# Up projection of a streaming-encoder block: channels by tokens against tokens by channels, with the result turned off TensorE

## The chip, the cores and the metric

The kernel runs on one core of one Trainium2 chip. The metric is device time in microseconds (us) of one execution. The kernel before was run three times: 1694.3, 1700.97 and 1701.85 us, median 1700.97 us. The profile shown here is of one further execution.

## The reference, cut to what matters

One layer (depth 1, batch 1) on 256 tokens of width 2048, all in float32. Three token mixers (a gated short convolution, a differential attention, a cross-attention into 256 memory tokens) are merged by gates and projected. Then comes the channel mixer, which the change is about:

```
x = x + rmsnorm(merged @ w_o, g_mix_post)

h = rmsnorm(x, g_ffn_pre)
u = causal_dwconv(h @ w_up, ffn_conv_w)        # w_up (2048, 11264), 3 taps over tokens, per channel
gate, val = split(u, 2, axis=-1)
x = x + rmsnorm((silu(gate) * val) @ w_down, g_ffn_post)   # w_down (5632, 2048)
```

The convolution runs along the tokens, so it wants channels on partitions and tokens along the free axis; the down projection wants its activations in that layout too, as the stationary operand.

## The kernel before, in words

**Blocks.** Every projection streams its weight through SBUF in blocks of 256 rows by 512 columns (512 KB). SP loads a block into one of four `raw` buffers (`load`, L283), once VectorE has finished with the block four places earlier (`lo_ready`). ScalarE rounds it to float32r into one of four `w_hi` buffers (`split`, L442), once TensorE is done with the block four places earlier (`block_done`). VectorE writes the rest, raw minus rounded, into `w_lo` (L750) and signals `lo_ready`. TensorE multiplies hi by hi, hi by lo and lo by hi. All four engines work through lists written out by hand; each list is in program order, and semaphores are the only coupling.

**Most stages** (`multiply`, L1148 to L1161): tokens are the stationary side (128 tokens by 128 of the inner dimension), the weight is the moving side, 512 columns. A block is 2 inner slices x 2 token tiles x 3 products = 12 matmuls of 512 columns. The result has tokens on partitions and is written to two PSUM banks of `ACC[0]` or `ACC[1]`.

**The up projection before** (`multiply_up`, L1409): the weight is the stationary side, 128 channels at a time, and the tokens move. A block is 2 inner slices x 4 channel blocks x 2 matmuls: one of 512 columns (weight hi against hi and lo of the 256 tokens, side by side in `hT_pair`), one of 256 columns (weight lo against hi). The result has channels on partitions, as the convolution wants it, in four banks: hi part and lo part side by side. The stage has 11 steps; a step is a gate half and a value half of 8 blocks each (512 channels each), 22 halves in all.

**What follows a half.** ScalarE copies one part out of PSUM (L679), VectorE adds the other (L995) and multiplies by the tokens' normalisation factors spread over all partitions (`r_row`, L997). ScalarE writes the third tap (`up_first_tap`, L684), VectorE adds the other two (`up_conv_taps`, L1004 and L1009). ScalarE applies silu to the gate, VectorE multiplies gate and value (`prod`, L1022), and the product is split into hi and lo for the down projection (L696, L1025). These calls stand between the splits of the following blocks: `value_done(j, i)` is called behind split i.

**The passage into the stage** (`last_chunk`, `first_gate`, `middle`): the new x needs the row sums of the whole w_o product, so the last w_o chunk is multiplied one token tile after the other from weights kept in SBUF. The first gate half is then computed in pieces (`tile`: 128-token pieces of three channel blocks, then the fourth, then the second token tile), while the 128x128 turns of the new x (`middle_turn`, L1329) and their splits go on. `spread_scale` (L1402) makes `r_row` with four small matmuls.

Of the kernel before, what the change touches and what calls it, by code (L numbers as in the profile page):

```python
# [11 lines left out]
P = 128  # L12
# [9 lines left out]
SPLIT = 4  # L22
MID = [(0, 0), (0, 1), (1, 0), (1, 1), (0, 2), (1, 2), (0, 3), (1, 3)]
# [3 lines left out]
def build_block_kernel(nc, x, mem, g_mix_pre, w_in, w_gate, b_gate, conv_w, w_conv_out,  # L27
# [47 lines left out]
    with ExitStack() as ctx:  # L75
# [68 lines left out]
        hT_pair = at("hT_pair", RA, [P, 2, DK, TOK], F32R)  # L144
        hT_hi, hT_lo = hT_pair[:, 0, :, :], hT_pair[:, 1, :, :]
        h2_pair, h2_hi, h2_lo = hT_pair, hT_hi, hT_lo
# [54 lines left out]
        up_scaled_sb = at("up_scaled_sb", RB + 88 * K, [P, BPC, TOK])  # L201
        r_diag = at("r_diag", RB + 96 * K, [P, NT, P])
        ones = at("ones", RB + 97 * K, [P, P])
        r_row = at("r_row", RB + 104 * K + 2 * K, [P, TOK])
        conv_g = at("conv_g", RB + 92 * K, [P, BPC, TOK])
        conv_v = at("conv_v", RB + 96 * K, [P, BPC, TOK])
        prod = at("prod", RB + 100 * K, [P, BPC, TOK])
# [5 lines left out]
        UP = [PS[:, 4 * h:4 * h + 4, :] for h in range(2)]  # L213
        MID_T = [PS[:, 4 + p % 4, :].rearrange("p (b t) -> p b t", t=P) for p in range(len(MID))]
        UP_A = [UP[h][:, :, 0:TOK] for h in range(2)]
        UP_B = [UP[h][:, :, TOK:2 * TOK] for h in range(2)]
# [35 lines left out]
        o_first, mix_last = sem("o_first"), sem("mix_last")  # L252
        mid_turned, mid_hi, mid_lo = (sem(n) for n in ("mid_turned", "mid_hi", "mid_lo"))
        r_diag_done, r_row_turned, r_row_done = (sem(n) for n in ("r_diag_done", "r_row_turned", "r_row_done"))
        up_scaled, up_conv = sem("up_scaled"), sem("up_conv")
        up_copied, up_summed = sem("up_copied"), sem("up_summed")
# [19 lines left out]
        def _(sp):  # L276
# [73 lines left out]
            with sp.Fori(0, NUP) as j:  # L350
                for i in range(CB):
                    load(N_UP + 2 * CB * j, i, w_up, i * KB, j * CW)
                for i in range(CB):
                    load(N_UP + 2 * CB * j, CB + i, w_up, i * KB, FF + j * CW)

            def down_chunk(j):
                for i in range(DB):
                    load(N_DN + DBV * j, i, w_down, i * KB, j * CW)
                    if i == 6 and isinstance(j, int):
# [69 lines left out]
        def _(act):  # L429
# [197 lines left out]
            def last_squares(t):  # L627

                if t == 0:
                    act.wait_ge(o_first, 1)  # L630
                else:
                    act.wait_ge(block_done, N_UP)
                act.wait_ge(mix_sq, NT * (NCH - 1) + 2 * t)
                nc.scalar.activation(junk[:], ACC[1][:, t, :], ACT.Square, accum_out=sq_part[:, t, NCH - 1:NCH]).then_inc(mix_sq, 1)

            def new_squares(t):

                act.wait_ge(x_new, NCH * (t + 1))
                act.wait_ge(mix_sq, NT * (NCH - 1) + 1 + 2 * t)
# [11 lines left out]
            def middle():  # L651
# [8 lines left out]
                split_kept(N_UP, 4)  # L660
                split_kept(N_UP, 5)
                new_squares(0)
                last_squares(1)
                split_kept(N_UP, 6)
                middle_hi(2)
                middle_hi(3)
                split_kept(N_UP, 7)
# [3 lines left out]
                act.wait_ge(r_row_turned, 1)  # L671
                nc.scalar.activation(r_row[:], PS[:, 4, 0:TOK], ACT.Copy).then_inc(r_row_done, 1)

            def up_copy(k, n_end, half):

                act.wait_ge(block_done, n_end)
                if not (isinstance(k, int) and k == 0):
                    act.wait_ge(up_conv, k)
                nc.scalar.activation(up_scaled_sb[:], UP_A[half], ACT.Copy).then_inc(up_copied, 1)  # L679

            def up_first_tap(k, dst, blk):
                act.wait_ge(up_scaled, k + 1)
                for b in range(BPC):
                    last = nc.scalar.activation(dst[:, b, :], up_scaled_sb[:, b, :], ACT.Copy, scale=up_taps[:, 2, bass.ds(blk + b, 1)])  # L684
                last.then_inc(tap0, 1)

            def value_done(j, i):

                if i == 2:
                    up_copy(2 * j + 1, N_UP + 2 * CB * j + 2 * CB, 1)  # L690
                if i == 4:
                    act.wait_ge(prod_done, AHEAD + j)
                    up_first_tap(2 * j + 1, conv_v, FK + BPC * j)
                if i == 7:
                    act.wait_ge(prod_done, AHEAD + j + 1)
                    nc.scalar.activation(act_hi[:, bass.ds(BPC * j, BPC), :], prod[:], ACT.Copy).then_inc(act_hi_done, 1)  # L696

            def up_step(j, jp):
# [3 lines left out]
                else:  # L702
                    for i in range(CB):
                        split(n, i)
                        value_done(jp, i)
                for i in range(CB):
                    split(n, CB + i)
                    if i == 2:
                        up_copy(2 * j, n + CB, 0)
                    if i == 4:  # L710
                        if jp is not None:
                            act.wait_ge(prod_done, AHEAD + j)
                        up_first_tap(2 * j, conv_g, BPC * j)
                    if i == 6:
                        act.wait_ge(up_conv, 2 * j + 1)
                        nc.scalar.activation(conv_g[:], conv_g[:], ACT.Silu).then_inc(silu_done, 1)
# [12 lines left out]
            def down_chunk(j, jp):  # L729
                for i in range(DB):  # L730
                    split(N_DN + DBV * j, i, down_landed(j, i), 1 if i < DB - 1 else 1 + DBV - DB)
                    if jp is None:
                        value_done(NUP - 1, i)
# [12 lines left out]
        def _(dve):  # L746
# [243 lines left out]
            def up_scale(k, half):  # L990

                dve.wait_ge(up_copied, k + 1)
                if isinstance(k, int) and k == 0:
# [486 lines left out]
```

## Time and profile before

| | |
|---|---|
| three runs | 1694.3, 1700.97, 1701.85 us, median 1700.97 |
| profiled execution | 1691.04 us, span 1689.2 us |
| TensorE busy | 1670.8 us (99%), granted clock 0.998 |
| VectorE, ScalarE busy | 1005.0 us (59%), 801.4 us (47%) |
| DMA | 320.90 MB, mean 190 GB/s, queue of SP 59.9% of 16 engines' span |

How to read it: the span runs from the first to the last instruction; the execution's own time lies 1.84 us above it. Matmuls overlap one another in the records, so a matmul's recorded duration is longer than the step from one to the next; the steps are read from start times. The up projection stretches from about 942 us to 1438 us of the span, the down projection from there to the end.

### The profile page before, as it was taken

The page shows a single profiled execution, that of the slowest core. Times are in us where ns is not written, and L with a number is a line of the kernel's source. Part 1 is how long each engine was busy: PE and PEld are TensorE (multiplying, and loading weights), DVE is VectorE, ACT ScalarE, POOL GpSimd, SP SyncE. Part 2 cuts the span into 40 slices and gives each one's busy share as a digit, 9 for nine tenths or more (in the row PEclk, how much of TensorE's full clock was granted, in tenths as well). Part 3 has the DMA queues.
Part 4 walks back from the last instruction along what each step waited for, and adds up shares of the span by engine and source line. Part 5 has one row for each costly group of instructions (what it writes and reads, how often), then busy time and mean ns, then how long its engine had stood idle before and what let it go on. Part 6 is the DMA issues. An engine that isn't in the chain of part 4 may idle for free.

```text
span 1689.2 us, 23203 instructions
## 1 busy us (share of the span) xinstructions
PE 1670.8 (99%) x8265; PEld 1408.2 (83%) x8265; DVE 1005.0 (59%) x1165; ACT 801.4 (47%) x1022; POOL 22.0 (1%) x51
## 2 busy tenths in 40 slices
PE   8999999999999999999999999999999999999997
PEld 7888888888888888888888888888888888888886
DVE  5554545544556656655555677777777777644544
ACT  6544444444444444444444555555555555443442
POOL 0000000000000000000000000000000000000000
PEclk9999999999999999999999999999999999999999
DMA  8556555666656655575656366666666665655653
GB/s 290 203 175 187 164 160 163 186 188 186 191 178 203 227 186 183 176 236 193 197 191 225 104 189 188 196 191 193 188 191 194 188 187 183 228 194 166 210 200 123
DMA packets 165792, 320.90 MB, mean 190 GB/s; under 512 B 10520, under 2 KB 11369, under 8 KB 165225
## 3 DMA queue, kind: packets, MB, share of 16 engines
q1 hardware_dynamic: 165705, 320.15, 59.9%
q8 instruction: 36, 0.59, 0.1%
q14 instruction: 19, 0.16, 0.0%
q10 hardware_dynamic: 32, 0.01, 0.0%
HBM read 318.02 MB, written 2.10 MB: 190 GB/s over the span
## 4 chain that ended last, share of the span: by engine, by line
PE 95%; DVE 2%; ACT 1%; issue 1%; DMA 1%; DVEq 0%; SPq 0%; POOL 0%; ACTq 0%
PE PS L1420 19%; PE PS L1158 18%; PE PS L1160 18%; PE PS L1159 18%; PE PS L1422 10%; PE PS L1310 3%; PE PS L1309 3%; PE PS L1308 3%; PE PS L1172 1%; ACT w_hi L442 0%; PE PS L1363 0%; PE PS L1250 0%; PE PS L1235 0%; DMA mem_sb<-in_mem_dram 0%; DVE y_down L1140 0%
## 5 line engine op out<-in xcount | busy, mean ns | idle before, releaser
L750 DVE TENSOR_TENSOR w_lo<-raw,w_hi 128x1024 fp32r<-128x1024 f32 x567 | 689.7, 1224 | 615.3 <-ACT w_hi L442 613.0
L442 ACT ACTIVATE w_hi<-raw 128x1024 fp32r<-128x1024 f32 x567 | 593.1, 1057 | 608.0 <-PE PS L1160 488.7
L1420 PE MATMUL PS<-hT_pair,w_hi 128*128 128x512 f32 x1376 | 477.4, 391 | 0.0
L1422 PE MATMUL PS<-hT_pair,w_lo 128*128 128x256 f32 x1376 | 385.3, 280 | 0.0
L1158 PE MATMUL PS<-w_hi,hT_pair 128*128 128x512 f32 x832 | 329.6, 396 | 0.0
L1160 PE MATMUL PS<-w_hi,hT_pair 128*128 128x512 f32 x832 | 324.4, 390 | 0.0
L1159 PE MATMUL PS<-w_lo,hT_pair 128*128 128x512 f32 x832 | 323.9, 389 | 0.0
L1420 PEld LDWEIGHTS PS<-hT_pair,w_hi 128*128 128x128 f32 x1376 | 257.3, 187 | 56.6 <-issue 0.2
L1422 PEld LDWEIGHTS PS<-hT_pair,w_lo 128*128 128x128 f32 x1376 | 260.1, 189 | 0.0
L1158 PEld LDWEIGHTS PS<-w_hi,hT_pair 128*128 128x128 f32 x832 | 156.3, 188 | 33.7 <-issue 2.7
L1160 PEld LDWEIGHTS PS<-w_hi,hT_pair 128*128 128x128 f32 x832 | 156.2, 188 | 33.1
L1159 PEld LDWEIGHTS PS<-w_lo,hT_pair 128*128 128x128 f32 x832 | 156.4, 188 | 31.2
L1158 PE MATMUL PS<-w_hi,act_hi 128*128 128x512 f32 x352 | 137.2, 390 | 0.0
L1160 PE MATMUL PS<-w_hi,act_lo 128*128 128x512 f32 x352 | 137.0, 389 | 0.0
L1159 PE MATMUL PS<-w_lo,act_hi 128*128 128x512 f32 x352 | 137.0, 389 | 0.0
L1158 PEld LDWEIGHTS PS<-w_hi,act_hi 128*128 128x128 f32 x352 | 66.1, 188 | 14.3 <-issue 0.6
L1160 PEld LDWEIGHTS PS<-w_hi,act_lo 128*128 128x128 f32 x352 | 66.1, 188 | 13.8
L1159 PEld LDWEIGHTS PS<-w_lo,act_hi 128*128 128x128 f32 x352 | 66.1, 188 | 13.6
L1158 PE MATMUL PS<-w_hi,memT_hi 128*128 128x512 f32 x128 | 50.7, 396 | 1.0 <-DVE up_taps L780 0.7
L1160 PE MATMUL PS<-w_hi,memT_lo 128*128 128x512 f32 x128 | 50.0, 390 | 0.0
L1159 PE MATMUL PS<-w_lo,memT_hi 128*128 128x512 f32 x128 | 49.8, 389 | 0.0
L679 ACT ACTIVATE up_scaled_sb<-PS 128x1024 f32<-128x1024 f32 x22 | 22.6, 1025 | 37.6 <-PE PS L1422 37.6
(210 smaller groups left out, 1397.1 us busy)
## 6 DMA issues: line engine op xcount, KB each, us to landing
raw<-in_w_up_dram SPq DMA_DIRECT2D x176, 512.0 KB, 3.9
raw<-in_w_in_dram SPq DMA_DIRECT2D x112, 512.0 KB, 3.7
raw<-in_w_gate_dram SPq DMA_DIRECT2D x96, 512.0 KB, 3.9
raw<-in_w_down_dram SPq DMA_DIRECT2D x88, 512.0 KB, 4.3
raw<-in_w_mem_kv_dram SPq DMA_DIRECT2D x32, 512.0 KB, 4.1
raw<-in_w_o_dram SPq DMA_DIRECT2D x32, 512.0 KB, 3.6
raw<-in_w_conv_out_dram SPq DMA_DIRECT2D x16, 512.0 KB, 3.5
raw<-in_w_cross_out_dram SPq DMA_DIRECT2D x16, 512.0 KB, 3.6
```

Source lines behind the costliest of these rows:

```text
L442: nc.scalar.activation(w_hi[i % RING][:], raw[i % RING][:], ACT.Copy).then_inc(hi_ready, inc)
L679: nc.scalar.activation(up_scaled_sb[:], UP_A[half], ACT.Copy).then_inc(up_copied, 1)
L750: nc.vector.tensor_tensor(w_lo[i % RING][:], raw[i % RING][:], w_hi[i % RING][:].bitcast(F32), ALU.subtract).then_inc(lo_ready, inc)
L1158: nc.tensor.matmul(o, a_hi, b_hi, start=first, stop=False)
L1159: nc.tensor.matmul(o, a_hi, b_lo, start=False, stop=False)
L1160: last = nc.tensor.matmul(o, a_lo, b_hi, start=False, stop=last_k)
L1172: last = nc.tensor.transpose(dst[:, b, t * P:(t + 1) * P], src[:, t, b * P:(b + 1) * P], ident[:])
L1308: nc.tensor.matmul(ACC[1][:, t, :], hi[:, k, s], w_hi[i % RING][:, c, :], start=k == 0, stop=False)
L1309: nc.tensor.matmul(ACC[1][:, t, :], hi[:, k, s], w_lo[i % RING][:, c, :], start=False, stop=False)
L1310: last = nc.tensor.matmul(ACC[1][:, t, :], lo[:, k, s], w_hi[i % RING][:, c, :], start=False, stop=k == HK - 1)
L1420: nc.tensor.matmul(o.rearrange("p (a t) -> p a t", a=2), b_hi, h2_pair[:, :, k, :], start=k == 0, stop=False, skip_group_check=True)
L1422: last = nc.tensor.matmul(o[:, 0:TOK], b_lo, h2_hi[:, k, :], start=False, stop=last_k, skip_group_check=True)
```

## The change

The up projection is multiplied as every other stage is (`multiply`: 12 matmuls of 512 columns a block, result with tokens on partitions, in `ACC[0]` for the gate and `ACC[1]` for the value). ScalarE takes a half out of PSUM in two instructions and applies the normalisation factor on the way, since it is now one number a partition (`up_evacuate`). To bring the channels onto the partitions, VectorE transposes 32x32 squares in place of the addition and the multiplication (`up_square`, two instructions a half), and SP moves the squares to where they belong: 16 DMAs a half (`move_squares`), each of 32 partitions x 8 x 128 bytes, from SBUF to SBUF. They are issued in four groups of four, each group behind one of the weight loads. Taps, silu and product follow one half later than before, and the product overwrites `conv_v`. `by_tile` now serves both the last w_o chunk and the first gate half: 128 tokens x 512 columns, token tile 0 over all 8 blocks, then token tile 1. `spread_scale`, `r_row` and the `SPLIT` pieces go. The diff, cut to its core:

```diff
@@ block.sync @@
-            with sp.Fori(0, NUP) as j:
-                for i in range(CB):
-                    load(N_UP + 2 * CB * j, i, w_up, i * KB, j * CW)
-                for i in range(CB):
-                    load(N_UP + 2 * CB * j, CB + i, w_up, i * KB, FF + j * CW)
+            def move_squares(j, half, a):
+                if a == 0:
+                    sp.wait_ge(up_squares, 2 * j + half + 1)
...
+                    if not (isinstance(j, int) and 2 * j + half == 0):
+                        sp.wait_ge(up_conv, 2 * j + half)
...
+                for m in range(P // SQ):
+                    sp.dma_start(turned_sb[SQ * m:SQ * (m + 1), :, SQ * a:SQ * (a + 1)],
+                                 squares_sb[SQ * a:SQ * (a + 1), :, SQ * m:SQ * (m + 1)]).then_inc(up_in[half], 16)
+            def up_step(j, jp):
+                for half in range(2):
+                    for i in range(CB):
+                        load(N_UP + 2 * CB * j, half * CB + i, w_up, i * KB, half * FF + j * CW)
+                        if jp is not None and i < P // SQ:
+                            move_squares(jp, half, i)
@@ block.scalar @@
-                nc.scalar.activation(up_scaled_sb[:], UP_A[half], ACT.Copy).then_inc(up_copied, 1)
+                for t in range(NT):
+                    last = nc.scalar.activation(up_stage[:, t, :], ACC[parity][:, t, :], ACT.Copy, scale=r_h2[:, t:t + 1])
+                last.then_inc(up_out, 1)
+            def up_first_tap(j, half, dst):
+                act.wait_ge(up_in[half], 16 * (P // SQ) ** 2 * (j + 1))
+                act.wait_ge(act_lo_done if half else prod_done, AHEAD + j)
...
+            def gate_done(j, i):
+                if i == 0:
+                    up_first_tap(j, 0, conv_g)
+                if i == 2:
+                    up_evacuate(2 * j + 1, N_UP + 2 * CB * (j + 1), 1)
@@ block.vector @@
-                nc.vector.tensor_tensor(up_scaled_sb[:], UP_B[half], up_scaled_sb[:], ALU.add).then_inc(up_summed, 1)
-                dve.wait_ge(up_summed, k + 1)
-                nc.vector.tensor_tensor(up_scaled_sb[:], up_scaled_sb[:], r_row[:, None, :].to_broadcast([P, BPC, TOK]),
-                                        ALU.mult).then_inc(up_scaled, 1)
+            def up_square(k):
+                dve.wait_ge(up_out, k + 1)
+                for t in range(NT):
+                    last = nc.vector.transpose(squares_sb[:, t:BPC * NT:NT, :], up_stage[:, t, :].rearrange("p (b n) -> p b n", n=P))
+                last.then_inc(up_squares, 1)
@@ block.tensor @@
+            def by_tile(n, a_hi, a_lo, acc, ready, after):
+                for t in range(NT):
+                    s = slice(t * P, (t + 1) * P)
+                    for i in range(CB):
...
+                            nc.tensor.matmul(acc[:, t, :], a_hi[:, k, s], b_hi, start=k == 0, stop=False)
+                            nc.tensor.matmul(acc[:, t, :], a_hi[:, k, s], b_lo, start=False, stop=False)
+                            last = nc.tensor.matmul(acc[:, t, :], a_lo[:, k, s], b_hi, start=False, stop=k == DK - 1)
...
-                    for i in range(CB):
-                        multiply_up(n, i, 0)
+                    for i in range(CB):
+                        multiply(n, i, CB, h2_hi, h2_lo, lambda t: ACC[0][:, t, :])
```

SP's list, where the last step's squares are moved during the first down chunk (the loop over the steps has the same pattern with w_up). Before:

```order
L283 DMA raw_49<-in_w_down_dram 128x2x512 [waits lo_ready]
L283 DMA raw_50<-in_w_down_dram 128x2x512 [waits lo_ready]
L283 DMA raw_51<-in_w_down_dram 128x2x512 [waits lo_ready]
L283 DMA raw_52<-in_w_down_dram 128x2x512 [waits lo_ready]
L283 DMA raw_49<-in_w_down_dram 128x2x512 [waits lo_ready]
```

and in the changed kernel, at the same place:

```order
L278 DMA raw_49<-in_w_down_dram 128x2x512 [waits lo_ready]
L356 DMA turned_sb<-squares_sb 32x8x32 [waits up_conv,up_squares]
L356 DMA turned_sb<-squares_sb 32x8x32 x3
L278 DMA raw_50<-in_w_down_dram 128x2x512 [waits lo_ready]
L356 DMA turned_sb<-squares_sb 32x8x32 x4
L278 DMA raw_51<-in_w_down_dram 128x2x512 [waits lo_ready]
L356 DMA turned_sb<-squares_sb 32x8x32 x4
L278 DMA raw_52<-in_w_down_dram 128x2x512 [waits lo_ready]
L356 DMA turned_sb<-squares_sb 32x8x32 x4
L278 DMA raw_49<-in_w_down_dram 128x2x512 [waits lo_ready]
```

Sixteen small DMAs now stand among four weight loads of 512 KB, on the one queue, behind four of every eight loads.

VectorE's list at the end of the stage (`w_lo<-raw,w_hi` is the split of a block). In the changed kernel, from the first split behind the loop:

```order
L777 TENSOR_TENSOR w_lo_58<-raw_50,w_hi_54 128x1024 [waits hi_ready]
L1028 SCALAR_TENSOR_TENSOR conv_g<-turned_sb,up_taps,conv_g 128x255 [waits tap0]
L1028 SCALAR_TENSOR_TENSOR conv_g<-turned_sb,up_taps,conv_g 128x255 x3
L1033 SCALAR_TENSOR_TENSOR conv_g<-turned_sb,up_taps,conv_g 128x254 [waits tap1]
L1033 SCALAR_TENSOR_TENSOR conv_g<-turned_sb,up_taps,conv_g 128x254 x3
L777 TENSOR_TENSOR w_lo_59<-raw_51,w_hi_55 128x1024 [waits hi_ready]
L777 TENSOR_TENSOR w_lo_60<-raw_52,w_hi_56 128x1024 [waits hi_ready]
L1021 STREAM_TRANSPOSE squares_sb<-up_stage 128x4x128 [waits up_out]
L1021 STREAM_TRANSPOSE squares_sb<-up_stage 128x4x128
L777 TENSOR_TENSOR w_lo_57<-raw_49,w_hi_53 128x1024 [waits hi_ready]
```

and before, a value half inside the loop and at the same splits:

```order
L750 TENSOR_TENSOR w_lo_60<-raw_52,w_hi_56 128x1024 [waits hi_ready]
L992 ISA
L995 TENSOR_TENSOR up_scaled_sb<-PS,up_scaled_sb 128x1024 [waits up_copied]
L997 TENSOR_TENSOR up_scaled_sb<-up_scaled_sb,r_row 128x1024 [waits up_summed]
L749 REGISTER_ALU
L750 TENSOR_TENSOR w_lo_57<-raw_49,w_hi_53 128x1024 [waits hi_ready]
L749 REGISTER_ALU
L750 TENSOR_TENSOR w_lo_58<-raw_50,w_hi_54 128x1024 [waits hi_ready]
L1002 REGISTER_ALU
L1004 ISA [waits tap0]
L1004 SCALAR_TENSOR_TENSOR conv_v<-up_scaled_sb,up_taps,conv_v 128x255
```

Before, the taps stood behind the sixth split of the half that follows their own, two splits behind the scaling. Now the squares stand behind the fourth split, and the taps behind the second split of the half after that.

## Rows read from the trace of the kernel before

**Rows 1.** The page: busy time of each engine, and the chain that ended last
```profile
PE 1670.8 (99%) x8265; PEld 1408.2 (83%) x8265; DVE 1005.0 (59%) x1165; ACT 801.4 (47%) x1022; POOL 22.0 (1%) x51
PE 95%; DVE 2%; ACT 1%; issue 1%; DMA 1%; DVEq 0%; SPq 0%; POOL 0%; ACTq 0%
```

**Rows 2.** Busy time in 980 to 1424: engines, then clock, DMA share, GB/s
```profile
980.00:1424.00 444.00, 444.00 (x2563) 391.49 (x2562) 324.57 (x380) 236.02 (x283) 0.00 (x0) 1.00 0.62 189
```

**Rows 3.** Timeline of TensorE: start, duration, line; first an up block, then a down block
```profile
1000.26 0.39 PE L1420 MATMUL PS<-hT_pair,w_hi 128*128 128x512 f32 x1
...
1003.04 0.39 PE L1420 MATMUL PS<-hT_pair,w_hi 128*128 128x512 f32 x1
...
1500.46 0.39 PE L1158 MATMUL PS<-w_hi,act_hi 128*128 128x512 f32 x1
...
1503.18 0.39 PE L1158 MATMUL PS<-w_hi,act_hi 128*128 128x512 f32 x1
```

**Rows 4.** The same view: last w_o chunk begins, value half 0 begins, down projection begins
```profile
919.94 0.39 PE L1344 MATMUL PS<-kept_hi,mixT_hi 128*128 128x512 f32 x1
...
972.45 0.47 PE L1420 MATMUL PS<-hT_pair,w_hi 128*128 128x512 f32 x1
...
1438.45 0.39 PE L1158 MATMUL PS<-w_hi,act_hi 128*128 128x512 f32 x1
```

**Rows 5.** The chain in order of time: one turn of the new x
```profile
949.61 0.45 PE PS L1329 x4
```

**Rows 6.** Waits of SP's queue in 980 to 1420: us, times, longest
```profile
SPq L282 <- DVE w_lo L750: 326.3, 159, 3.8
```

**Rows 7.** Timelines of ScalarE and VectorE around the taps of value half 0
```profile
1000.78 1.72 ACT L684 ACTIVATE conv_v<-up_scaled_sb,up_taps 128x256 f32<-128x256 f32 x4 [2.03 <-DVE up_scaled_sb L997]
...
1003.48 1.23 DVE L750 TENSOR_TENSOR w_lo<-raw,w_hi 128x1024 fp32r<-128x1024 f32 x1 [1.72 <-ACT w_hi L442]
1004.62 1.66 DVE L1004 SCALAR_TENSOR_TENSOR conv_v<-up_scaled_sb,up_taps,conv_v 128x255 f32<-128x255 f32 x4
1006.43 1.67 DVE L1009 SCALAR_TENSOR_TENSOR conv_v<-up_scaled_sb,up_taps,conv_v 128x254 f32<-128x254 f32 x4
1008.01 1.22 DVE L750 TENSOR_TENSOR w_lo<-raw,w_hi 128x1024 fp32r<-128x1024 f32 x1
1009.15 1.22 DVE L1022 TENSOR_TENSOR prod<-conv_g,conv_v 128x1024 f32<-128x1024 f32 x1
1010.28 1.22 DVE L750 TENSOR_TENSOR w_lo<-raw,w_hi 128x1024 fp32r<-128x1024 f32 x1
```

**Rows 8.** Groups by line: busy, mean ns of one
```profile
L442 ACT ACTIVATE w_hi<-raw 128x1024 fp32r<-128x1024 f32 x567 | 593.1, 1057 | 608.0 <-PE PS L1160 488.7 <-PE PS L1422 63.9 <-PE PS L1310 39.6
L1033 DVE TENSOR_TENSOR y_mix<-PS,g_post 128x512 f32<-128x512 f32 x2 | 1.4, 680 | 0.0
```

**Rows 9.** Timeline of SP: issues in the stage and at the start
```profile
1002.01 0.37 SPq L283 DMA_DIRECT2D raw<-in_w_up_dram  x1
...
6.96 0.42 SPq L293 DMA_DIRECT2D vec_rows<-in_g_ffn_pre_dram  x1
7.42 0.44 SPq L293 DMA_DIRECT2D vec_rows<-in_conv_w_dram  x1
...
9.82 0.60 SPq L296 DMA_DIRECT2D lam_rows<-in_lambda_k_dram  x1
10.46 0.60 SPq L296 DMA_DIRECT2D lam_rows<-in_lambda_q_dram  x1
```

**Rows 10.** DMA issues by line: count, KB each, median us from issue to landing
```profile
out_dram<-y_down SPq DMA_DIRECT2D x8, 256.0 KB, 2.2
```

**Rows 11.** DMA answers for 16.25 to 16.5 us, then for 22 to 24 us
```profile
DMA packets 47, 0.02 MB, mean 86 GB/s; under 512 B 41, under 2 KB 41, under 8 KB 47
q1 hardware_dynamic: 47, 0.02, 30.2%
...
DMA packets 397, 0.78 MB, mean 392 GB/s; under 512 B 21, under 2 KB 21, under 8 KB 396
q1 hardware_dynamic: 396, 0.77, 102.0%
```

More of the change, by code:

```diff
@@ L670, in middle, with up_evacuate @@
                 new_squares(1)
-                act.wait_ge(r_row_turned, 1)
-                nc.scalar.activation(r_row[:], PS[:, 4, 0:TOK], ACT.Copy).then_inc(r_row_done, 1)
-            def up_copy(k, n_end, half):
+            def up_evacuate(k, n_end, parity):
                 act.wait_ge(block_done, n_end)
-                if not (isinstance(k, int) and k == 0):
-                    act.wait_ge(up_conv, k)
-                nc.scalar.activation(up_scaled_sb[:], UP_A[half], ACT.Copy).then_inc(up_copied, 1)
@@ L681, in up_first_tap @@
-            def up_first_tap(k, dst, blk):
-                act.wait_ge(up_scaled, k + 1)
+                if isinstance(k, int) and k == 0:
+                    act.wait_ge(rms_ready, 5)
+                else:
+                    act.wait_ge(up_squares, k)
+                for t in range(NT):
[4 more added lines that the diff above has]
+                act.wait_ge(act_lo_done if half else prod_done, AHEAD + j)
@@ L1003, in up_conv_taps @@
                 for b in range(BPC):
-                    last = nc.vector.scalar_tensor_tensor(out=dst[:, b, 1:TOK], in0=up_scaled_sb[:, b, 0:TOK - 1], scalar=taps(1, b),
+                    last = nc.vector.scalar_tensor_tensor(out=dst[:, b, 1:TOK], in0=turned_ch[:, b, 0:TOK - 1], scalar=taps(1, b),
                                                           in1=dst[:, b, 1:TOK], op0=ALU.mult, op1=ALU.add)
@@ L1086, in middle @@
                 nc.vector.tensor_copy(sq_mix[:], sq_h2[:]).then_inc(h2_sq, 1)
-                dve.wait_ge(rms_ready, 5)
-                nc.vector.memset(ones[:], 1.0)
-                for t in range(NT):
-                    last = nc.vector.tensor_scalar(r_diag[:, t, :], ident[:], r_h2[:, t:t + 1], None, ALU.mult)
-                last.then_inc(r_diag_done, 1)
             def up_step(j, jp):
@@ new lines, in by_tile, with last_chunk, after, ready @@
+                            last.then_inc(first_tile, 1)
+                        after(t, i)
+            def last_chunk():
+                def after(t, i):
+                    if t and i >= 3 and i < 7:
+                        middle_turn(i - 3)
+                pe.wait_ge(evacuated[1], E_O + 1)
+                by_tile(N_O + CB * (NCH - 1), mixT_hi, mixT_lo, ACC[1], lambda t, i: None, after)
+            def first_gate():
+                def ready(t, i):
+                    pe.wait_ge(mid_lo, NCH * t + i // 2 + 1)
+                def after(t, i):
+                    if (t, i) in ((0, 5), (0, 7), (1, 0), (1, 1)):
+                        middle_turn(4 + ((0, 5), (0, 7), (1, 0), (1, 1)).index((t, i)))
+                pe.wait_ge(evacuated[0], E_UP)
+                by_tile(N_UP, h2_hi, h2_lo, ACC[0], ready, after)
@@ L1400, in _ @@
                         turn_merged(T_MERGE + NCH - 1)
-            def spread_scale():
-                pe.wait_ge(r_diag_done, 1)
-                for t in range(NT):
-                    last = nc.tensor.matmul(PS[:, 4, t * P:(t + 1) * P], ones[:], r_diag[:, t, :], start=True, stop=True)
-                last.then_inc(r_row_turned, 1)
-            def multiply_up(n, i, half, hi=None, lo=None):
-                hi, lo = (hi, lo) if hi is not None else (w_hi[i % RING], w_lo[i % RING])
-                pe.wait_ge(lo_ready, n + i + 1)
-                for c in range(KB):
-                    k = KB * i + c
-                    for b in range(BPC):
-                        s = slice(b * P, (b + 1) * P)
-                        o, last_k = UP[half][:, b, :], k == DK - 1
-                        b_hi, b_lo = hi[:, c, s], lo[:, c, s]
-                        nc.tensor.matmul(o.rearrange("p (a t) -> p a t", a=2), b_hi, h2_pair[:, :, k, :], start=k == 0, stop=False,
-                                         skip_group_check=True)
-                        last = nc.tensor.matmul(o[:, 0:TOK], b_lo, h2_hi[:, k, :], start=False, stop=last_k, skip_group_check=True)
-                last.then_inc(block_done, 1)
             def up_step(j, jp):
```

193 lines of the change are left out of this document (77 added, 116 removed).

## The prediction

> **What bounds the kernel now.** I read the page's busy times and its chain first: TensorE is busy for 99% of the span, and 95% of the chain that ended last is TensorE [rows 1]. Then the busy times of the stage that changes: from 980 to 1424 us TensorE never pauses (444.00 of 444.00 us, at the full granted clock), the DMA engines are 62% busy, VectorE 324.6 and ScalarE 236.0 us of the 444 [rows 2]. So only what shortens TensorE's own list can gain, and whatever keeps it waiting is a loss. Then the timelines, for the step from one matmul to the next (the recorded durations overlap): a block of the up projection takes 1003.04 - 1000.26 = 2.78 us in four channel blocks twice, and a block in the form that the change brings, read in the down projection, takes 1503.18 - 1500.46 = 2.72 us [rows 3]. Over the whole stage the old form comes to (1438.45 - 972.45) / 21 = 22.19 us a half [rows 4]; the new one would be 8 x 2.72 = 21.76. SP spends 326 of 440 us waiting for VectorE to free a raw buffer, 159 times [rows 6]: it always has time, as long as nothing is put into its list.
>
> **What goes and what it frees.** (1) 21 halves x (22.19 - 21.76) = 9.0 us on TensorE. The columns are the same (6144 a block); what goes is four matmuls of 16. (2) The passage: from the start of the last w_o chunk to value half 0 TensorE now takes 972.45 - 919.94 = 52.5 us [rows 4]. In the new form it is 16 blocks x 2.72 = 43.5, and eight turns at 0.45 [rows 5] = 3.6, together 47.1, if no piece waits. Token tile 1 of the last chunk (10.9 us) and tile 0 of the gate half (10.9 us) cover the norm and the turns of the other tile, about as now. So 5.4 us; between 0 (if the new order waits for its turns) and 5.4. (3) VectorE's addition and multiplication and ScalarE's wide copy cost nothing today, since TensorE doesn't wait for them, and their successors (two evacuations, two transposes a half) are shorter than they. Sum of the gains: 14.4 us, the most that this change can give: 1691.0 - 14.4 = 1676.6 us.
>
> **What is added, and where it lies.** A half's result now goes through SP. Look for the loop: SP may issue the first load of a half H+1 only when VectorE has split block 4 of half H (counting from 0), since that frees the raw buffer. Behind this load stand the first four moves, then load, four moves, twice more and once more: 20 issues until the last move of that group is out. They carry the half that was multiplied before H. When they have landed, ScalarE writes the third taps (behind split 0 of half H+1), then splits block 1; VectorE splits block 1, adds the taps, splits block 2, (in a value half) makes the product, splits block 3, transposes the squares of the half just done, splits block 4. That frees the next round of loads. Nothing of TensorE is in this round. Where it is longer than 21.76 us, TensorE waits for the splits in every half. Its length, from rows:
> - SP: four loads at 0.37 and sixteen moves at 0.42, each with the 0.04 from one issue to the next (6.96 + 0.42 against 7.42) [rows 9]: 1.64 + 7.36 = 9.0. The moves have no row. The nearest small DMA (16 rows from HBM) took 0.42 to 0.44, the weight load, which has as many separate runs (256), 0.37, the broadcast rows of 32 KB 0.60. I take 0.42; ends 0.37 and 0.60.
> - Landing: the shortest row from issue to landing is 2.2 us for stores from SBUF [rows 10]. Without their data (8 packets of 82 ns an engine, below: 0.66), with 0.2 for the move's own and without the 0.46 already counted: 1.3.
> - ScalarE: taps 1.72 [rows 7], split 1.06 [rows 8].
> - VectorE: split to taps 1004.62 - 1003.48 = 1.14; both taps 1008.01 - 1004.62 = 3.39; split 1.14; product 1.13 in every second half, so 0.57; split 1.14 [rows 7]; two instructions for the squares at the 0.68 of a 512-column instruction [rows 8] = 1.36 (not in the trace; ends 0.34 and 1.22 each, the halves and the 1024-column time); split 1.22.
> - Four handoffs between engines or dependent instructions, 0.1 each (one reads 6.43 - 4.62 - 1.66 = 0.15 [rows 7]): 0.4.
>
> Sum: 9.0 + 1.3 + 1.72 + 1.06 + 1.14 + 3.39 + 1.14 + 0.57 + 1.14 + 1.36 + 1.22 + 0.4 = 23.4 us. That is 1.7 above TensorE's 21.76 and 1.3 above today's 22.19. Over 21 halves 21 x (23.44 - 22.19) = +26; less the 5.4 of the passage +21: 1691.0 + 21 = 1712 us. The waits of ScalarE and VectorE for the moved data are in it: behind ScalarE's wait stand the splits of blocks 1 to 3, which VectorE and TensorE need, and the evacuation.
>
> Ends: with 0.37 for a move the round is 22.6, the sum +4; with 0.60 it is 26.3, the sum +81. With squares at 0.34 each -14, at 1.22 +23.
>
> **The moved bytes in the DMA engines.** A move has 256 runs of 128 bytes, 16 an engine, 64 in a group. At full load 397 packets, nearly all of 2 KB, filled 102% of 16 x 2 us: about 82 ns each; at 16.25 us, where the broadcast rows pass, 47 packets took 30.2% of 16 x 0.25 = 1.21 us; less six of 82 ns leaves 0.72 us for 41 small ones, 17 ns each, though 4 us of engine time went by, some 85 ns a small packet with the gaps [rows 11]. A group of a load and four moves is 16 x 82 = 1.31 us plus 64 packets an engine; SP needs 0.41 + 4 x 0.46 = 2.25 for it. So the engines set the pace from 15 ns a packet. The 41 are of 256 bytes and semaphore writes; 128 bytes between SBUF and SBUF should be below 17, an estimate of 13. At 17 the sum is +15 us more; at 85 the group is 6.8 us.
>
> Here the Trainium skill speaks on both sides. "DMA: Bandwidth & Descriptors", section Specifications, puts the least size for full rate at 512 bytes and says that below it the engine reads, modifies and writes; that is the second rival's mechanism. Its section "Why small descriptors are slow (HBM only)" says that copies between SBUF and SBUF are spared. By the first the group would go past SP's 2.25 us and the time to that rival's; by the second the sum above stands. The rows show 17 ns for small packets, without a penalty that could be seen in the transfer itself, and an unexplained gap between them.
>
> **The rivals.**
> - *TensorE keeps the pace.* If a move issues like a load (0.37), lands faster, or the squares take half as long, the round falls to 21.8 or less and all 14.4 us are kept: 1677 us. For it: SP has 326 us to spare, and each term has an end that is lower. Against: it needs two or three of them at once. The point from which it decides is a round of 21.76 us. This is the case on the other side: faster.
> - *The small packets hold the rings.* Between 17 and 85 ns a packet; at 40 the group is 1.31 + 2.56 = 3.87 us, 1.62 over SP's, four groups 6.5 us a half, 21 halves +136: 1712 + 136 = 1848 us. At 85 it is 2090. For it: the gap in rows 11. Against: those packets came from HBM, many from one and the same row.
> - *The issue is slow.* Moves at 0.60, as the broadcast rows: 1691 + 81 = 1772 us. For it: the same size, 32 KB. Against: at that time many loads stood in the queue.
>
> **How the numbers follow.** The profiled execution (1691.04) lies 9.9 us below the median of the three runs (1700.97), so each time is set 10 us higher for a median: forecast 1712 becomes 1722, the rivals 1687, 1858 and 1782. Chances: forecast 0.50 (its own range 1700 to 1765), TensorE keeps the pace 0.14, the rings 0.21, the issue 0.13, something else 0.02. A change of up to 0.5% (8.5 us) can't be told from none. Of the forecast's 0.50 about 0.14 falls into that band (a round of 22.0 to 22.8), of the first rival 0.03. So faster 0.12, same 0.17, slower 0.71. The range: 1688 leaves out most of the first rival, 1830 the upper half of the rings' case.
>
> **What would show it.** In the new profile the stage's TensorE steps should be 0.2267 us inside a block, with idle time before the matmuls of blocks 1 to 3 of each half, put down to `w_lo`; the chain should run through SP's issues, landings of `turned_sb`, L707 and the taps. VectorE should wait for ScalarE's taps there, and ScalarE for the landing of `turned_sb`. If the issue row of the moves reads 0.42 and the landing 1.8, the sum stands; if DMA share in the stage is above 90%, the rings are the bound; if TensorE's idle time is under 5 us, the first rival holds. The passage from the first L1369 to value half 0 should be 47.1 us. I am wrong if the stage's halves are 21.8 us, or over 25.

## The result, and the profile after

The changed kernel takes 1808.1 us (median of four runs, 1806.1 to 1808.8) against 1697.6 for the kernel before: ratio 1.0655, 95% interval 1.0624 to 1.0687, so 6.2 to 6.9% slower. The four runs of the kernel before lie between 1692.9 and 1701.9 us. The forecast was 1722 us: the direction was right, the loss about five times as large.

First the page of the changed kernel: span, busy times, two of the 40-slice rows, chain, and the issue row of the moves.

```profile
span 1806.9 us, 22044 instructions
PE 1701.8 (94%) x7493; PEld 1391.1 (77%) x7493; DVE 976.4 (54%) x1162; ACT 827.9 (46%) x1062; POOL 22.0 (1%) x51
...
PE   8999999999999999999999888889888898899997
...
DMA  7566556666556655655565667666666676655653
...
PE 68%; SPq 11%; DVE 10%; issue 5%; ACT 3%; DMA 3%; DVEq 1%; ACTq 0%
...
turned_sb<-squares_sb SPq DMA_DIRECT2D x352, 32.0 KB, 2.8
```

TensorE has fallen from 99 to 94% busy and from 95 to 68% of the chain [rows 1]; what it lost, SP's queue (11%), VectorE (10%), ScalarE and the landings have. The holes lie in the stage of the up projection alone (slices 23 to 35), and the DMA engines aren't full there (6 to 7 tenths). The waits of the changed kernel (engine, line, what it waits for: us, times, longest):

```profile
DVE w_lo L777 <- ACT w_hi L461: 759.3, 390, 10.6
...
PE PS L1184 <- DVE w_lo L777: 87.4, 30, 5.3
ACT conv_v L707 <- DMA turned_sb<-squares_sb: 95.2, 11, 9.1
ACT conv_g L707 <- DMA turned_sb<-squares_sb: 86.4, 11, 9.1
```

TensorE waits for `w_lo`, VectorE for ScalarE (up to 10.6 us), and ScalarE for `turned_sb`, in all 22 halves and 8.3 us on average. That is the round that the prediction described. One turn of it, in a value half: first SP's timeline (start, duration, line, count), then ScalarE's, then VectorE's.

```profile
1111.40 3.83 SPq L278 DMA_DIRECT2D raw<-in_w_up_dram  x3
1115.48 2.57 SPq L356 DMA_DIRECT2D turned_sb<-squares_sb  x4
1118.39 0.39 SPq L278 DMA_DIRECT2D raw<-in_w_up_dram  x1
1118.82 2.56 SPq L356 DMA_DIRECT2D turned_sb<-squares_sb  x4
1121.73 0.38 SPq L278 DMA_DIRECT2D raw<-in_w_up_dram  x1
1122.15 2.57 SPq L356 DMA_DIRECT2D turned_sb<-squares_sb  x4
1125.06 0.39 SPq L278 DMA_DIRECT2D raw<-in_w_up_dram  x1
1125.49 2.56 SPq L356 DMA_DIRECT2D turned_sb<-squares_sb  x4
```

```profile
1129.96 1.70 ACT L707 ACTIVATE conv_v<-turned_sb,up_taps 128x256 f32<-128x256 f32 x4 [9.14 <-DMA turned_sb<-squares_sb]
1131.57 1.99 ACT L461 ACTIVATE w_hi<-raw 128x1024 fp32r<-128x1024 f32 x2
```

```profile
1112.22 1.29 DVE L1021 STREAM_TRANSPOSE squares_sb<-up_stage 128x512 f32<-128x512 f32 x2
1113.44 2.31 DVE L777 TENSOR_TENSOR w_lo<-raw,w_hi 128x1024 fp32r<-128x1024 f32 x2
...
1132.64 1.23 DVE L777 TENSOR_TENSOR w_lo<-raw,w_hi 128x1024 fp32r<-128x1024 f32 x1 [10.57 <-ACT w_hi L461]
1133.79 1.66 DVE L1028 SCALAR_TENSOR_TENSOR conv_v<-turned_sb,up_taps,conv_v 128x255 f32<-128x255 f32 x4
...
1140.58 1.30 DVE L1021 STREAM_TRANSPOSE squares_sb<-up_stage 128x512 f32<-128x512 f32 x2
```

Read it as a ring. Squares at 1112.22; split 4 frees a buffer, and the load in front of the first move is issued at 1115.23 - 0.38 = 1114.85; the last move is out at 1128.05; the tap starts at 1129.96; the next squares at 1140.58. So 2.63 + 13.20 + 1.91 + 10.62 = 28.36 us. Squares start 44 times between 972.7 and 1557.2, two a half 0.6 apart: (1556.6 - 972.7) / 21 = 27.80 us a half (the turn above is a value half; the gate halves have no product and are shorter). The forecast of this round was 23.4.

The step is 3.34 us from one load with its four moves to the next. Four moves are out in 2.56 + 0.04, that is 0.65 each where the forecast had 0.46, and SP pauses 0.35 before each load behind them. This pause isn't made by the moves. In a loop SP runs four short instructions before every load (a register sum at L275, the semaphore at L277, two register instructions at L278), and the kernel before has them too: three loads of its down loop take 1.78 us, so (1.78 - 3 x 0.37) / 2 = 0.33 lie between two of them. In the first down chunk of the changed kernel, whose list is written out, the load follows the moves after 0.05, but then holds SP for 0.60 where it was 0.38 (first line from the kernel before, then two from the changed one):

```profile
1490.36 1.78 SPq L283 DMA_DIRECT2D raw<-in_w_down_dram  x3
...
1532.72 2.58 SPq L356 DMA_DIRECT2D turned_sb<-squares_sb  x4
1535.35 0.60 SPq L278 DMA_DIRECT2D raw<-in_w_down_dram  x1
```

### The profile page after: what moved, and what is told of

Its sections match the earlier page's. It is cut to its first block, busy times and chain, and to the rows that moved or that the text cites. A ratio compares the mean times of both kernels' runs of the same rounds, so it can differ in the third digit from the quotient of the medians.

```text
span 1806.9 us, 22044 instructions
## 1 busy us (share of the span) xinstructions
PE 1701.8 (94%) x7493; PEld 1391.1 (77%) x7493; DVE 976.4 (54%) x1162; ACT 827.9 (46%) x1062; POOL 22.0 (1%) x51
## 4 chain that ended last, share of the span: by engine, by line
PE 68%; SPq 11%; DVE 10%; issue 5%; ACT 3%; DMA 3%; DVEq 1%; ACTq 0%
PE PS L1184 18%; PE PS L1186 18%; PE PS L1185 18%; SPq L356 9%; DVE w_lo L777 3%; PE PS L1336 2%; PE PS L1335 2%; PE PS L1334 2%; DMA turned_sb<-squares_sb 2%; ACT w_hi L461 2%; SPq L278 2%; PE PS L1198 1%; DVE conv_v L1028 1%; PE PS L1371 1%; PE PS L1369 1%
## 5 line engine op out<-in xcount | busy, mean ns | idle before, releaser
L1184 PE MATMUL PS<-w_hi,hT_hi 128*128 128x512 f32 x1504 | 608.2, 404 | 78.8 <-DVE w_lo L777 78.8
L1185 PE MATMUL PS<-w_lo,hT_hi 128*128 128x512 f32 x1504 | 597.6, 397 | 0.0
L1186 PE MATMUL PS<-w_hi,hT_lo 128*128 128x512 f32 x1504 | 596.9, 397 | 0.0
L1184 PEld LDWEIGHTS PS<-w_hi,hT_hi 128*128 128x128 f32 x1504 | 289.6, 193 | 154.9 <-DVE w_lo L777 93.5
L1186 PEld LDWEIGHTS PS<-w_hi,hT_lo 128*128 128x128 f32 x1504 | 289.5, 192 | 62.5
L1185 PEld LDWEIGHTS PS<-w_lo,hT_hi 128*128 128x128 f32 x1504 | 290.1, 193 | 58.4
L707 ACT ACTIVATE conv_v<-turned_sb,up_taps 128x256 f32<-128x256 f32 x44 | 18.8, 497 | 95.2 <-DMA turned_sb<-squares_sb 95.2
L1184 PE MATMUL PS<-w_hi,mixT_hi 128*128 128x512 f32 x96 | 37.5, 390 | 0.0
L1186 PE MATMUL PS<-w_hi,mixT_lo 128*128 128x512 f32 x96 | 37.4, 389 | 0.0
L1185 PE MATMUL PS<-w_lo,mixT_hi 128*128 128x512 f32 x96 | 37.4, 389 | 0.0
```

The costliest lines, as they stand in the source:

```text
L707: last = nc.scalar.activation(dst[:, b, :], turned_ch[:, b, :], ACT.Copy, scale=up_taps[:, 2, bass.ds(half * FK + BPC * j + b, 1)])
L1184: nc.tensor.matmul(o, a_hi, b_hi, start=first, stop=False)
L1185: nc.tensor.matmul(o, a_hi, b_lo, start=False, stop=False)
L1186: last = nc.tensor.matmul(o, a_lo, b_hi, start=False, stop=last_k)
```

## The experiments

Ratios are against runs of the kernel before made beside each run (medians 1692.6 to 1693.3 us). "Round" is worked out in every run as above, from the first and the last squares. If all time lost is the round's excess over TensorE's 21.76 us, the time must be 1679 + 21 x (round - 21.76), where 1679 is the first run below:

| run | round, us | that gives | measured, us | ratio, 95% |
|---|---|---|---|---|
| no moves | 21.76 | | 1679.0 | 0.988 to 0.995 |
| 8 moves, light loads | 22.58 | 1696 | 1696.4 | 0.999 to 1.003 |
| one buffer, taps later | 24.05 | 1727 | 1724.7 | 1.014 to 1.021 |
| 8 moves | 24.62 | 1739 | 1740.7 | 1.023 to 1.030 |
| moves by GpSimd | 25.74 | 1763 | 1765.5 | 1.038 to 1.046 |
| 12 moves | 26.33 | 1775 | 1776.1 | 1.044 to 1.051 |
| small moves | 26.95 | 1788 | 1788.3 | 1.052 to 1.059 |
| long packets | 27.19 | 1793 | 1794.2 | 1.056 to 1.063 |
| 16 moves, light loads | 27.42 | 1798 | 1800.4 | 1.058 to 1.066 |
| waits filled | 27.74 | 1805 | 1806.3 | 1.062 to 1.070 |
| the changed kernel | 27.80 | 1806 | 1808.1 | 1.062 to 1.069 |
| late taps, two buffers | 21.76 | 1679 | 1679.2, 1678.1 | 0.987 to 0.993 (second set) |

The rule holds within 3 us in every run. It says where the time is lost, in the round and nowhere else. What remained was what makes the round that long.

**Without the moves.**

```diff
-                for m in range(P // SQ):
-                    sp.dma_start(turned_sb[...], squares_sb[...]).then_inc(up_in[half], 16)
-                act.wait_ge(up_in[half], 16 * (P // SQ) ** 2 * (j + 1))
+                act.wait_ge(up_squares, 2 * j + half + 1)
```

> This kernel leaves out the 16 transfers of each half: the first tap waits for VectorE's squares only, and reads a buffer that GpSimd sets once, so the taps work on constants. All other instructions of the changed kernel stay. If the transfers and the way they hang the round together are the whole loss (my theory, whichever of their costs it is), TensorE keeps its pace of 21.8 us a half and the time is the ceiling of the prediction's sum: about 14 us below the kernel before, 1680 to 1690. If the loss came from the other new work (squares on VectorE, evacuation with a scale on ScalarE, matmuls by tokens), 1760 or more remains.

1679.0 us, 13.6 below the kernel before. The whole loss is the moves and what they tie together; evacuation, squares and matmuls by tokens cost nothing on the path. It is also the ceiling of the gains, forecast as 14.4.

**Count, packets or bytes.** Two kernels with 16 moves a half of another content (first the small moves, then the long packets).

```diff
-    turned_sb[SQ * m:SQ * (m + 1), :, SQ * a:SQ * (a + 1)],  squares_sb[SQ * a:SQ * (a + 1), :, SQ * m:SQ * (m + 1)]
+    turned_sb[SQ * m:SQ * (m + 1), 0:1, SQ * a:SQ * (a + 1)],  squares_sb[SQ * a:SQ * (a + 1), 0:1, SQ * m:SQ * (m + 1)]
+    turned_sb[SQ * m:SQ * (m + 1), 2 * a:2 * a + 2, :],  squares_sb[SQ * a:SQ * (a + 1), 2 * m:2 * m + 2, :]
```

> Each of the 16 transfers of a half carries one of its eight 128-byte columns of squares, so 32 packets of 128 bytes and not 256; the other seven parts of what the taps read are constants, so the channels come out different. Number, place and waits of the transfers stay. Theory 1 (SyncE is held about 0.65 us by each transfer, whatever it carries): a half stays near 27 us, 1795 to 1810. Theory 2 (what counts is the packets, in the rings or in the time that SyncE needs to write them out): transfers fall to a load's 0.39 us or less, the round to 23 us or less, TensorE nearly keeps pace: 1690 to 1725.

> Each of the 16 transfers of a half moves the same 32 KB between the same partitions, but as 32 packets of 1 KB (a contiguous piece of each row) and not 256 of 128 bytes; the elements land in other places of the row, so the channels are mixed. Theory 1 (time by the number of transfers): 1795 to 1810. Theory 2 (time by the number of packets): 1690 to 1725. If the small transfers of the other run are quick and these are not, it is the bytes.

1788.3 and 1794.2 us: both just under the 1795 to 1810 of theory 1, and over 60 us above theory 2. An eighth of the packets brings 20 us of 110, and whether those carry 128 bytes or 1 KB changes 6. The issue rows (min/median/max ns; small moves, long packets, changed kernel):

```profile
L357 SPq DMA_DIRECT2D turned_sb<-squares_sb x352: 507/590/1303, 976.0 to 1553.0; - x176
```

```profile
L356 SPq DMA_DIRECT2D turned_sb<-squares_sb x352: 507/590/1649, 975.7 to 1558.1; - x176
```

```profile
L356 SPq DMA_DIRECT2D turned_sb<-squares_sb x352: 585/610/1535, 976.4 to 1572.8; - x176
```

SP is held some 0.6 us by such a DMA almost whatever it carries. The case in which packets hold the rings falls.

**Twelve moves, and eight.** `for m in range(P // SQ - 1)` and `for m in range(0, P // SQ, 2)` in the move loop.

> The changed kernel with 12 of the 16 transfers of a half (those to quadrants 0 to 2; quadrant 3 keeps constants). Theory 1: 27.4 - 4 x 0.65 = 24.8 us a half, 1679 + 21 x 3.0 = 1742, 1735 to 1760. Rival (fixed parts): over 1780.

> The changed kernel with 8 of the 16 transfers of a half (those to partition quadrants 0 and 2; the others' rows keep constants, so half of the channels come out different), the rest and all waits unchanged. Theory 1 (each transfer holds SyncE 0.65 us in the round): 27.4 - 8 x 0.65 = 22.2 us a half, just over TensorE's 21.8: 1679 + 21 x 0.4 = 1687, 1682 to 1695. Rival (a fixed part, such as the landing or the four pauses behind the groups, makes most of it): over 1720.

1776.1 and 1740.7 us: both outside what my theory gave, and the one with 8 moves where I had put the rival. From 16 moves to 8 the time falls by 67.4 us, so a move is worth 67.4 / 8 / 21 = 0.4 us of the round, not 0.65. Where does the rest go? SP's timeline with 8 moves, then the tap that waits for them:

```profile
1099.96 0.37 SPq L279 DMA_DIRECT2D raw<-in_w_up_dram  x1
1100.58 1.27 SPq L357 DMA_DIRECT2D turned_sb<-squares_sb  x2
1102.18 0.39 SPq L279 DMA_DIRECT2D raw<-in_w_up_dram  x1
...
1106.67 1.25 SPq L357 DMA_DIRECT2D turned_sb<-squares_sb  x2
```

```profile
1111.90 1.71 ACT L710 ACTIVATE conv_v<-turned_sb,up_taps 128x256 f32<-128x256 f32 x4 [5.98 <-DMA turned_sb<-squares_sb]
```

SP is through after 7.96 us, 5.2 sooner, as forecast; but the tap comes 1111.90 - 1107.92 = 3.98 us behind the last move, not 1.91 (with 12 moves 3.1). While SP issues, loads of 512 KB every 2.05 us ask for 256 GB/s, every 3.34 us for 157; the mean of this kernel in 1050 to 1450 us is 182. So it may be that the quicker SP issues, the more of the loads' bytes is still on its way when the last move comes. Two more runs tested this new theory.

**Loads of half the size.** All else as in the kernel with 8 moves and as in the changed kernel.

```diff
-                sp.dma_start(raw[i % RING][:], cols(w, k0, c0))
+                sp.dma_start(raw[i % RING][:, :, 0:width], cols(w, k0, c0)[:, :, 0:width])   # up stage: width = CW // 2
```

> The kernel with 8 transfers a half, with every weight load of the up stage after the first gate half cut to half its bytes (256 of 512 columns, 256 KB; the other half of the raw tile keeps old weights, so the products come out different). Number and order of all DMAs and all waits stay. With 8 transfers SyncE was done 5.2 us sooner, but ScalarE's tap came 4.0 us behind the last transfer's issue and not 1.9. Theory 3 (the transfers of a half stand behind its loads in the same rings: issued 2.05 us apart, four loads of 512 KB are not through when the last transfer is issued, issued 3.34 us apart they are): with loads of half the size the tap comes 1.9 us behind again, a half takes 24.7 - 2.1 = 22.6 us, and the time is 1741 - 21 x 2.1 = 1697, 1688 to 1710. Rival (the landing has a fixed floor of about 4 us for other reasons): 1730 to 1745.

> The changed kernel with all 16 transfers of a half and with weight loads of half the bytes, as in the other run of this call. Theory 3 with theory 1: here SyncE's issue paces the loads at 3.34 us and the rings are nearly empty when the last transfer comes, so lighter loads give little: 0 to 0.6 us a half, 1795 to 1810. Rival (the rings' bytes are what paces SyncE's issue of 0.65 us or the landing here too): 1780 or less.

1696.4 and 1800.4 us, both as expected. With 8 moves and light loads the last move is out at 1095.81 and the tap starts at 1097.61, 1.8 us behind, SP's pace being the same:

```profile
1094.56 1.25 SPq L357 DMA_DIRECT2D turned_sb<-squares_sb  x2
```

```profile
1097.61 1.71 ACT L710 ACTIVATE conv_v<-turned_sb,up_taps 128x256 f32<-128x256 f32 x4 [3.83 <-DMA turned_sb<-squares_sb]
```

So two terms of the round trade against each other: SP's issue of the moves, and the wait of the last move behind the loads. In the changed kernel the first is by far the larger, and loads of half the size bring only 8 us.

**The round or the transfers.** The kernel before, with 16 moves of the same form put into SP's list at the same places in 20 of the 22 halves, between memory that no one needs.

```diff
+                        if moved and i < P // SQ:
+                            idle_moves(j, half, i)      # waits only for the landing of the moves of the half before
```

> The kernel before, with 16 transfers a half added on SyncE's queue in 20 of its 22 halves, of the changed kernel's form (32 partitions, 256 packets of 128 bytes) and at its places, four behind each of a half's first four loads. They copy between memory that no one needs, and nobody waits for them but SyncE itself, for those of the half before. Theory 1 (it is the round, not the transfers): SyncE has 13.2 us more in a half of 22.2 and the loads slip by less than the ring has: within 0.5% of the kernel before. Rival (the queue or the rings are short): loads come late, 1720 or more.

1692.7 us, ratio 0.9997 (0.9974 to 1.0019). Sixteen moves a half on SP's queue and in the rings are free as long as nothing that feeds the next ones waits for them.

**Fewer instructions in the round.** The taps stand behind split 2 and the product behind split 4; landing buffer and waits stay.

```diff
-                if i == 0:
+                if i == 2:
                     up_first_tap(j, 0, conv_g)
...
-                if i == 1:
+                if i == 2:
                     up_conv_taps(2 * j, conv_g, ...)
```

> The changed kernel with one landing buffer and all its waits, but the taps later in the half: ScalarE's first tap after its split 2 (was 0), VectorE's taps after its split 2 (was 1), the product after split 4 (was 2), what hangs on them moved likewise. The round stays closed and only three instructions leave it: ScalarE's split 1 (1.06), VectorE's splits 1 and 2 (1.15 and 1.14), and on every second half the product (1.13, so 0.57 a half): 27.4 less 3.9 makes 23.5 us a half. Theory 1 (the half is the sum of the round): 1679 + 21 x (23.5 - 21.8) = 1715, 1700 to 1725. Rival (the transfers' issue and the loads behind them set the half, whatever stands after them): it stays within 10 us of 1808.

1724.7 us, at the upper edge of what was expected: the round lost 3.7 us of the 3.9.

**The moves on another queue.**

```diff
+            def move_squares(j, half):                  # @block.gpsimd
+                pool.wait_ge(up_squares, 2 * j + half + 1)
...
+                        pool.dma_start(turned_sb[...], squares_sb[...]).then_inc(up_in[half], 16)
```

> The changed kernel with the same 16 transfers a half issued by GpSimd, which is idle in this stage, and not by SyncE; waits as before, no load stands between them or behind them. The round loses four loads with their gaps (2.8) and split 4 (1.2). Theory 1 gives the time by what GpSimd needs to issue one: at SyncE's 0.65 us the round is 27.4 - 4.0 = 23.4 and the time 1679 + 21 x 1.6 = 1713; at 1.0 us it is 29 and the time 1830. Rival (the loads held up behind the transfers are what costs): with the loads free, 1680 to 1695 whatever GpSimd needs up to 1 us each.

1765.5 us, between my two cases, although GpSimd issues faster than SP: at SP's 0.65 us a move I had expected 1713. Its transfers land later (page of this kernel: queue's packets and MB, then KB and median us to landing; then timelines of GpSimd and ScalarE):

```profile
q0 software_dynamic: 11264, 11.56, 2.4%
...
turned_sb<-squares_sb POOLq DMA_DIRECT2D x352, 32.0 KB, 4.6
```

```profile
1103.74 9.19 POOL L430 DMA_DIRECT2D turned_sb<-squares_sb  x16 [16.49 <-DVE squares_sb L1018]
```

```profile
1118.06 1.71 ACT L704 ACTIVATE conv_v<-turned_sb,up_taps 128x256 f32<-128x256 f32 x4 [7.14 <-DMA turned_sb<-squares_sb]
```

Sixteen issues take 9.2 us and no load stands between them, but the tap starts 1118.06 - 1112.93 = 5.1 us behind the last (4.5 on average over the halves). How much of that is this queue and how much the loads beside it wasn't separated.

**The clock.** In the changed kernel the granted clock falls to its lower level behind TensorE's waits: the step between matmuls goes from 0.227 us (2.4 GHz) to 0.427 (1.2 GHz; start, duration, line):

```profile
1133.92 0.68 PE L1184 MATMUL PS<-w_hi,hT_hi 128*128 128x512 f32 x1 [3.33 <-DVE w_lo L777]
1134.40 0.63 PE L1185 MATMUL PS<-w_lo,hT_hi 128*128 128x512 f32 x1
1134.82 0.63 PE L1186 MATMUL PS<-w_hi,hT_lo 128*128 128x512 f32 x1
...
1137.67 0.39 PE L1184 MATMUL PS<-w_hi,hT_hi 128*128 128x512 f32 x1
1137.90 0.39 PE L1185 MATMUL PS<-w_lo,hT_hi 128*128 128x512 f32 x1
```

```diff
                         multiply(n, i, CB, h2_hi, h2_lo, lambda t: ACC[0][:, t, :])
+                        if i == 0:
+                            fill()          # 14 matmuls of 512 columns into PS[:, 6]
```

> The changed kernel with 14 more matmuls of 512 columns (3.2 us at the full clock) between block 0 and block 1 of every half but the first two, into a PSUM bank that no one reads: TensorE works where it waited, and its clock should stay at 2.4 GHz. Theory 1 (the round has no TensorE in it, so the slow clock after each wait costs nothing): 1800 to 1815. Rival (the slow clock adds 1.6 to 3 us a half to the path): 35 to 60 us less, 1750 to 1775.

1806.3 us. The clock in 1050 to 1500 us is 1.00 instead of 0.93 (second and first row), and nothing is won:

```profile
1050.00:1500.00 450.00, 384.52 (x1547) 307.34 (x1548) 243.92 (x314) 214.94 (x262) 0.00 (x0) 0.93 0.64 169
```

```profile
1050.00:1500.00 450.00, 412.29 (x1774) 330.56 (x1775) 243.80 (x315) 214.90 (x262) 0.00 (x0) 1.00 0.65 169
```

The slow clock was an effect of the waits; TensorE isn't in the round, so it only waited less when it worked more slowly.

**The round opened.** Gate and value halves land in buffers of their own (the second lies in the last 4 KB of `act_lo`, free until the last step), the taps move behind split 3 and 4, and the squares wait for the landing, no longer for the taps.

```diff
+                    dve.wait_ge(up_in[1 - half], 16 * (P // SQ) ** 2 * (j + half))   # up_square
...
-                        sp.wait_ge(up_conv, 2 * j + half)                            # move_squares
...
-                if i == 0:
+                if i == 3:
                     up_first_tap(j, 0, conv_g)
```

> All 16 transfers stay as they are, with 128-byte packets. Only the round is opened: gate and value halves land in buffers of their own, ScalarE's first tap comes after its split 3 and VectorE's taps after its split 4 of the half, where they were at split 0 and 1, and what hangs on them moves by 3; the squares wait for the landing of the transfers before, not for the taps. So splits 1 to 3 and the squares no longer stand behind the taps. Theory 1 (the loss is the closed round: 13.2 us of SyncE, landing, taps, splits, one after the other): squares, split, SyncE and landing make 18.5 us in a row, under TensorE's 21.8, and the time falls below the kernel before, to 1680 to 1690. Rival (rings or SyncE's queue are short as such): weight loads come late behind the transfers in any order, and the time stays over 1720.

1679.2 us, and 1678.1 in a second set of runs (ratio 0.987 to 0.993, so 0.7 to 1.3% faster than the kernel before), with all 352 moves in it. SP still needs 3.34 us from one load with its moves to the next, but a half now takes 21.76 us, and TensorE doesn't pause. Three things changed at once; what the second buffer brings without the later taps was not run (timeline of SP; then engines, clock, DMA share, GB/s in 1050 to 1400, with and without moves):

```profile
1110.67 0.39 SPq L278 DMA_DIRECT2D raw<-in_w_up_dram  x1
1111.10 2.56 SPq L352 DMA_DIRECT2D turned_g<-squares_sb  x4
1114.01 0.38 SPq L278 DMA_DIRECT2D raw<-in_w_up_dram  x1
```

```profile
1050.00:1400.00 350.00, 350.00 (x1546) 289.82 (x1545) 243.21 (x305) 214.75 (x257) 0.00 (x0) 1.00 0.80 217
```

```profile
1050.00:1400.00 350.00, 350.00 (x1546) 289.82 (x1545) 242.61 (x305) 216.66 (x260) 0.00 (x0) 1.00 0.65 193
```

## Why the prediction was right and wrong

- **TensorE bounds the kernel, and the gain.** Right: (1425.98 - 969.02) / 21 = 21.76 us a half in the run with late taps, as worked out; the gains together measured 13.6 of the 14.4.
- **The passage.** Right: 969.11 - 921.74 = 47.4 us in the changed kernel, forecast 47.1.
- **The round exists and sets the pace.** Right, with its members in the order given. That is shown by the run without moves and by the idle moves.
- **Its length, 23.4 us.** Wrong by 4.4, and this is the step that failed. 21 x 4.4 = 92, where the profiled execution (1808.7 us) lies 97 above the 1712 forecast for it; the medians lie only 86 apart, because the 10 us that I had added for a median weren't there. By terms: SP 13.2 against 9.0; landing 1.9 against 1.3; everything on ScalarE and VectorE, handoffs included, 27.80 - 13.20 - 1.91 = 12.7 against 13.1.
- **SP's term** is the one mis-sized. I took 0.42 + 0.04 a move from small transfers out of HBM, because they were the nearest by kind; the row of the same size, 0.60 for the broadcast 32 KB [rows 9], had the right value. I gave that case 0.13 and explained its row by a full queue, which nothing showed. But the size isn't the reason either: moves of 4 KB held SP for 0.59. The case's time, 1782, left out the pauses before the loads. No row of mine had them, but the trace of the kernel before did, 0.33 each (above). The term in full: 16 x (0.65 - 0.46) for the moves, 3 x (0.35 - 0.04) for the pauses and 0.25 - 0.04 in front of the first move make 4.2 us, of which the last two are 1.1, or 24 us in 21 halves.
- **Landing** was wrong in kind too: counted as a fixed 1.3, it depends on how many bytes of loads SP has issued just before. Had SP been as quick as I forecast (2.25 us a group), it would have been between the 3.1 and 4.0 of the runs with 12 and 8 moves, and the forecast still too low: with 8 moves SP takes 8.0, less than my 9.0, and the round is 24.6.
- **Squares** 0.69 an instruction, forecast 0.68. Right.
- **The packets in the rings.** The rival had 0.21 and was wrong. The moves raise the DMA share from 0.65 to 0.80: 0.15 x 16 x 21.76 = 52 us of engine time a half for 4096 packets, 12.7 ns each, where my estimate was 13. The section "Why small descriptors are slow (HBM only)" of the Trainium skill's page "DMA: Bandwidth & Descriptors" says that copies between SBUF and SBUF are spared. These runs agree with it in part: by the 82 ns of a 2 KB packet, 128 bytes would take 82 / 16 = 5.1 ns, so a small packet costs 2.5 times its bytes, but far less than the 40 ns that the rival needed. The 20 us between small and full moves are mostly SP's 0.61 against 0.65. The prediction's +15 us for packets of 17 ns should read 84 x (2.40 - 2.25) = 13.
- **The range** (1688 to 1830) held the time, but thanks to a case that was wrong.

## What to carry to other kernels

A DMA's price is first the time that its issuing queue is held, some 0.6 us for a move of 32 partitions within SBUF, with 4 KB as with 32; count DMAs before bytes. In a loop add the instructions that stand before each DMA, 0.33 us here. The issue costs nothing while it stands beside the work, and all of it once it stands in a ring of buffers: list the ring (who frees what for whom), add up its members, and compare with the engine that should set the pace. If it is longer, don't shorten its members first; give the landing a second buffer and take the consumers later, which here turned +6.5% into -1%.

## What the runs showed of the hardware

- A DMA from SBUF to SBUF is issued by SP in 0.59 us (32 packets) or 0.61 (256 packets), both medians, against 0.38 for a load of 512 KB. GpSimd needs 0.582, but its transfers land after 4.6 us (median) instead of 2.8. Its queue carried the 11.5 MB of the moves in 5632 packets of 2 KB and as many of 4 bytes, where SP's data packets were of 128 bytes.
- How long a load of 512 KB holds SP depends on what stands in front: 0.37 us behind a pause, 0.47 directly behind another load (the run with late taps, first down chunk), 0.60 directly behind a move. In a loop four short instructions stand before each load and make a pause of 0.33 to 0.35, behind a load as behind 2, 3 or 4 moves; written out it is 0.04 to 0.05.
- A short DMA lands later the more bytes were issued just before it: the tap starts 1.9, 3.1 and 4.0 us behind the last move's issue with loads every 3.34, 2.7 and 2.05 us (means over the halves 1.8, 3.0 and 3.8), and 1.8 at the last pace with loads of half the size. Whether the order in the queue or the shared DMA engines make it wait wasn't separated.
- Behind a wait of 3.3 us the granted clock fell to 1.2 GHz for some 3.4 us; that cost nothing where the wait was for others.
